# Forgetting attention before the second output projection: values of a head one step later, weight splits in halves, output parts in another order

## What is computed

```python
def fox_mixer(q_raw, k_raw, v_raw, f_raw, f_bias, norm_gain):
    """logit[t,s] = q_t.k_s/sqrt(d) + sum_{s<j<=t} log f_j, s <= t."""
    ...
    def block(i):
        ...
        logits = jnp.einsum('bhtd,bhsd->bhts', qb, k) + (cb[..., :, None] - cum[..., None, :])
        logits = jnp.where(mask, logits, NEG_INF)
        p = jax.nn.softmax(logits, axis=-1)
        return jnp.einsum('bhts,bhsd->bhtd', p, v)
    ...
    o = rms_norm(o, norm_gain)
```

## Time and profile before

| | us |
|---|---|
| median of 3 runs (1623.51 to 1626.19) | 1625.05 |
| the profiled execution | 1622.29 |
| its span | 1621.1 |

### The profile page before, as it was taken

The page is one execution under the profiler, slowest core; times in us unless marked ns, Lnnn a source line. Parts: engine busy times, 40 slices in busy tenths (PEclk is TensorE's granted clock), DMA queues, the critical chain, the costliest instruction groups (busy, mean ns, idle before and its releaser), DMA issues.

```text
span 1621.1 us, 17534 instructions
## 1 busy us (share of the span) xinstructions
PE 1482.9 (91%) x6907; PEld 1160.5 (72%) x6907; DVE 1024.0 (63%) x1354; ACT 756.7 (47%) x995; POOL 121.8 (8%) x143
## 2 busy tenths in 40 slices
PE   6999989889989999999999999999889699999981
PEld 5776668668667787888878787885547578888861
DVE  4888875564325654355546568736434788898976
ACT  5553444644334322122223442254344677887753
POOL 0500000000000000000000303100000011111012
PEclk8989999899999999999999999999999799999996
DMA  6212132202103342322123221111005599999974
GB/s 209 81 67 71 71 130 79 79 28 102 53 26 117 130 137 72 106 104 104 62 72 114 90 93 53 53 53 53 0 1 194 211 374 414 405 411 413 406 294 181
DMA packets 39329, 231.57 MB, mean 143 GB/s; under 512 B 4400, under 2 KB 5696, under 8 KB 17104
## 3 DMA queue, kind: packets, MB, share of 16 engines
q1 hardware_dynamic: 30640, 200.09, 33.0%
q0 software_dynamic: 7648, 27.87, 4.7%
q10 hardware_dynamic: 960, 2.49, 0.4%
HBM read 213.66 MB, written 16.78 MB: 142 GB/s over the span
## 4 chain that ended last, share of the span: by engine, by line
PE 75%; DVE 12%; ACT 6%; issue 4%; DMA 2%; POOL 0%; POOLq 0%; ACTq 0%; DVEq 0%
PE bank L416 15%; PE bank L417 14%; PE bank L418 14%; PE bank L2956 5%; PE bank L2958 5%; PE bank L2957 5%; PE bank L562 3%; DVE w_lo L372 2%; PE bank L435 1%; PE bank L2207 1%; ACT w_hi L366 1%; PE bank L2236 1%; PE bank L437 1%; PE bank L436 1%; PE bank L802 1%
## 5 line engine op out<-in xcount | busy, mean ns | idle before, releaser
L416 PE MATMUL bank<-h_hi,w_hi 128*128 128x512 f32 x952 | 390.5, 410 | 25.8 <-DVE h_lo L496 13.6
L417 PE MATMUL bank<-h_lo,w_hi 128*128 128x512 f32 x952 | 379.9, 399 | 0.0
L418 PE MATMUL bank<-h_hi,w_lo 128*128 128x512 f32 x952 | 379.3, 398 | 0.0
L372 DVE TENSOR_TENSOR w_lo<-w_raw,w_hi 128x2048 fp32r<-128x2048 f32 (+3 forms) x89 | 196.5, 2208 | 96.1 <-ACT w_hi L366 95.5
L416 PEld LDWEIGHTS bank<-h_hi,w_hi 128*128 128x128 f32 x952 | 182.6, 192 | 80.4 <-issue 16.2
L418 PEld LDWEIGHTS bank<-h_hi,w_lo 128*128 128x128 f32 x952 | 182.3, 192 | 42.7
L417 PEld LDWEIGHTS bank<-h_lo,w_hi 128*128 128x128 f32 x952 | 182.6, 192 | 40.6 <-issue 1.9
L366 ACT ACTIVATE w_hi<-w_raw 128x2048 fp32r<-128x2048 f32 (+3 forms) x89 | 158.4, 1780 | 64.8 <-PE bank L418 64.8
L3136 DVE TENSOR_TENSOR h_lo<-w_raw,h_hi 128x2048 fp32r<-128x2048 f32 x32 | 73.3, 2292 | 15.4 <-ACT h_hi L3037 15.4
L3136 DVE TENSOR_TENSOR lo_b<-raw_b,hi_b 128x2048 fp32r<-128x2048 f32 x32 | 73.2, 2288 | 8.7 <-ACT hi_b L3037 8.6
L416 PE MATMUL bank<-a_hi,w_hi 128*128 128x512 f32 x176 | 70.4, 400 | 4.5 <-DVE a_lo L1648 4.5
(11 more groups left out here) (577 smaller groups left out, 2765.1 us busy)
## 6 DMA issues: line engine op xcount, KB each, us to landing
w_raw<-in_params_dram SPq DMA_DIRECT2D x122, 1024.0 KB, 4.9
raw_b<-in_params_dram SPq DMA_DIRECT2D x51, 1024.0 KB, 8.3
w_raw<-in_params_dram SPq DMA_DIRECT2D x16, 704.0 KB, 4.0
result_rows<-osb POOLq DMA_DIRECT2D x16, 512.0 KB, 8.2
result_rows<-prm POOLq DMA_DIRECT2D x8, 512.0 KB, 3.1
xt<-in_x_t_dram POOLq DMA_DIRECT2D x1, 2048.0 KB, 9.3
scratch_rows<-htm SPq DMA_DIRECT2D x4, 512.0 KB, 3.0
out_dram<-pr SPq DMA_DIRECT2D x4, 512.0 KB, 2.6
```

What stands on the lines that cost most here:

```text
L372: V.tensor_tensor(k.w_lo[:, g % SPLIT, 0:size], k.raw[:, g % RAW, 0:size], k.w_hi[:, g % SPLIT, 0:size].bitcast(F32), ALU.subtract).then_i ...
L416: PE.matmul(ps, wh, hi[:, c, 0:width], start=c == 0, stop=False)
L417: PE.matmul(ps, wh, lo[:, c, 0:width], start=False, stop=False)
L418: m = PE.matmul(ps, wl, hi[:, c, 0:width], start=False, stop=c == parts - 1)
```

## The change

- The values of head h (now `pe_fox_out`) move from the end of step 4h + 5 into step 4h + 6, behind that step's scores; those of the last head stand behind one eighth of the output projection, where they had stood ahead of it. What depends on them moves along: ACT's squares and copy of a pair of heads go from the end of step 8j + 9 to step 8j + 10, behind the exponential; PE's sum one step later, ACT's copy of it too.
- Three weight slots are split in two halves, the halves one step apart: `fvb` on DVE (steps 4 and 5; ACT still takes it whole), and the first two slots of `w_out2` on both engines (ACT steps 8, 9 and 19, 20; DVE 10, 11 and 21, 22).
- At the end, ACT takes the exponentials of the first three pairs right after the last `fpt`, ahead of the squares of the last pair; DVE scales three, makes three low parts, and then scales the last. Between exponentials and logarithm ACT's tables are exchanged twice more.
- `pe_w_out2` takes parts in the order (blocks, part) 01:4, 01:5, 01:6, 23:4, 01:7, 23:5, 23:6, 23:7, where it had 01:4 to 01:7 and then 23:4 to 23:7.
- `dve_residual_input(k, 1)` moves from `dve_mix_in` to `dve_hgrn`, ahead of the split of slot `fqb`.

The matmuls, their shapes and all sums are the same.

```diff
+def act_split_half(k, g, half):
+    A, s, n = k.nc.scalar, k.s, SIZES[g] // 2
+    if half == 0:
+        A.wait_ge(k.w_load[g % RAW], 16 * (g // RAW + 1))
+        A.wait_ge(s.gemm, FINAL_BLOCK[g - SPLIT] + 1)
+    m = A.activation(k.w_hi[:, g % SPLIT, half * n:half * n + n], k.raw[:, g % RAW, half * n:half * n + n], ACT.Copy)
+    if half:
+        m.then_inc(s.w_hi, 1)
...
@@ dve_mix_in
     dve_exponents(k, 1)
-    dve_residual_input(k, 1)
     dve_keys(k, 1)
@@ dve_hgrn
     V.tensor_tensor(w1, w1, qf, ALU.mult).then_inc(s.hg_wk, 1)
+    dve_residual_input(k, 1)
     dve_split_to(k, SLOT0["fqb"])
@@ pe_fox
+        if step >= 6 and step % TT == 2:
+            pe_fox_out(k, step // TT - 1)
...
-        if step in (10, 18, 26):
+        if step in (11, 19, 27):
             pe_fox_sum(k, step // 8 - 1)
...
-            if t == TT - 1:
...
-    pe_w_out2_half(k, 12, 2)
+    pe_w_out2_half(k, 12, 1)
+    pe_fox_out(k, FX_H - 1)
+    pe_w_out2_half(k, 13, 1)
+    pe_w_out2_half(k, 14, 1)
     pe_fox_sum(k, 3)
-    pe_w_out2_half(k, 14, 2)
+    pe_w_out2_half(k, 15, 1)
@@ act_fox
+            if step in (10, 18, 26):
+                act_fox_squares(k, step // 8 - 1)
...
-            act_split_to(k, SLOT0["w_out2"] + 1)
-        if step in (11, 19, 27):
+            act_split_half(k, SLOT0["w_out2"] + 1, step - 19)
+        if step in (12, 20, 28):
...
+    a.own()
+    for j in range(3):
+        A.activation(k.grs[:, j, :], k.grs[:, j, :], ACT.Exp, scale=-0.5).then_inc(s.gn_rs, 1)
+    act_fox_squares(k, 3)
+    act_mixed_hi(k, 4)
+    act_mixed_hi(k, 5)
     A.wait_ge(s.gn_sum, 8)
     a(A.activation(k.grs[:, 3, :], k.bank[7][:, :], ACT.Ln, bias=k.eps[:, 0:1], scale=1.0 / HD))
     a.own()
...
+    act_mixed_hi(k, 6)
+    A.activation(k.grs[:, 3, :], k.grs[:, 3, :], ACT.Exp, scale=-0.5).then_inc(s.gn_rs, 1)
     act_mixed_hi(k, 7)
@@ dve_fox
-    dve_fox_scale(k, 0)
-    for j in range(1, 4):
+    for j in range(3):
         dve_fox_scale(k, j)
-        dve_mixed_lo(k, 4 + j - 1)
+    for j in range(3):
+        dve_mixed_lo(k, 4 + j)
+    dve_fox_scale(k, 3)
     dve_mixed_lo(k, 7)
@@ pe_w_out2
-    for b0 in (0, 2):
-        for c in range(4, DB):
+    for b0, c in ((0, 4), (0, 5), (0, 6), (2, 4), (0, 7), (2, 5), (2, 6), (2, 7)):
...
```

More of the change, by code:

```diff
@@ L372, in dve_split, with dve_split_half @@
     V.tensor_tensor(k.w_lo[:, g % SPLIT, 0:size], k.raw[:, g % RAW, 0:size], k.w_hi[:, g % SPLIT, 0:size].bitcast(F32), ALU.subtract).then_inc(s.w_lo, 1)
+def act_split_half(k, g, half):
+    A, s, n = k.nc.scalar, k.s, SIZES[g] // 2
+    assert k.act_slot == g
+    if half == 0:
[4 more added lines that the diff above has]
+        m.then_inc(s.w_hi, 1)
+        k.act_slot += 1
+    else:
+        k.a(m)
+def dve_split_half(k, g, half):
+    V, s, n = k.nc.vector, k.s, SIZES[g] // 2
+    assert k.dve_slot == g
+    if half == 0:
+        V.wait_ge(s.w_hi, g + 1)
+    at = slice(half * n, half * n + n)
+    m = V.tensor_tensor(k.w_lo[:, g % SPLIT, at], k.raw[:, g % RAW, at], k.w_hi[:, g % SPLIT, at].bitcast(F32), ALU.subtract)
+    if half:
+        m.then_inc(s.w_lo, 1)
+        k.dve_slot += 1
+    else:
+        k.v(m)
 def act_split_to(k, g):
@@ L2188, in pe_w_out2_half, with pe_fox_out @@
     pe_fm(k, "w_out2", q // 8, q // 4 % 2, k.hi, k.lo, after="sp", first=q % 4, stop=q % 4 + n)
+def pe_fox_out(k, h):
+    PE, s = k.nc.tensor, k.s
+    r0, blk = HD * (h % 2), h // 2
+    PE.wait_ge(s.sm_pt, SM0 + TT * h + TT)
+    if h % 2 == 0 and blk:
+        PE.wait_ge(s.hg_sig, 6 + blk)
+    if h in (0, 4):
+        PE.wait_ge(s.evac_a, EMPTIED[BLOCK0["fvb" if h else "fva"] + 3][1])
+    for j in range(TT):
+        m = PE.matmul(k.bank[7][r0:r0 + HD, j * P:T], k.fv[:, j, h * HD:h * HD + HD], k.fpt[:, h % 2, j, j * P:T],
+                      start=j == 0, stop=j == TT - 1, skip_group_check=True)
+    m.then_inc(s.fx_o, 1)
 def pe_fox(k):
@@ L2227, in pe_fox @@
             m.then_inc(s.sm_t, 1)
-            if t == TT - 1:
-                r0, blk = HD * (h % 2), h // 2
-                PE.wait_ge(s.sm_pt, SM0 + i + 1)
-                if h % 2 == 0 and blk:
-                    PE.wait_ge(s.hg_sig, 6 + blk)
-                if h in (0, 4):
-                    PE.wait_ge(s.evac_a, EMPTIED[BLOCK0["fvb" if h else "fva"] + 3][1])
-                for j in range(TT):
-                    m = PE.matmul(k.bank[7][r0:r0 + HD, j * P:T], k.fv[:, j, h * HD:h * HD + HD], k.fpt[:, h % 2, j, j * P:T],
-                                  start=j == 0, stop=j == TT - 1, skip_group_check=True)
-                m.then_inc(s.fx_o, 1)
-    pe_w_out2_half(k, 12, 2)
+    pe_w_out2_half(k, 12, 1)
+    pe_fox_out(k, FX_H - 1)
+    pe_w_out2_half(k, 13, 1)
+    pe_w_out2_half(k, 14, 1)
     pe_fox_sum(k, 3)
-    pe_w_out2_half(k, 14, 2)
+    pe_w_out2_half(k, 15, 1)
 def act_fox_squares(k, j):
@@ L2305, in act_fox @@
     a.own()
-    for j in range(4):
-        A.activation(k.grs[:, j, :], k.grs[:, j, :], ACT.Exp, scale=-0.5).then_inc(s.gn_rs, 1)
-        if j:
-            act_mixed_hi(k, 4 + j - 1)
+    act_mixed_hi(k, 6)
+    A.activation(k.grs[:, 3, :], k.grs[:, 3, :], ACT.Exp, scale=-0.5).then_inc(s.gn_rs, 1)
     act_mixed_hi(k, 7)
@@ L2359, in dve_fox @@
                 V.tensor_tensor(in_two(k.hk[:, b, :]), in_two(k.hk[:, b, :]), k.hg[b], ALU.mult).then_inc(s.hg_gate, 1)
[L2360 to L2363 removed]
+        elif step in (4, 5):
+            if step == 5:
+                dve_mix(k, "fkb", 0, k.fk[:, 2, :])
+            dve_split_half(k, SLOT0["fvb"], step - 4)
         elif step in (6, 7, 8):
@@ L2424, in pe_w_out2 @@
     PE, s = k.nc.tensor, k.s
-    for b0 in (0, 2):
-        for c in range(4, DB):
-            for b in (b0, b0 + 1):
-                pe_fm(k, "w_out2", b // 2, b % 2, k.hi, k.lo, first=c, stop=c + 1, after="sp" if b == 0 else None)
-            if b0 and c in (5, 6):
-                pe_w_out2_turn(k, c - 5)
+    for b0, c in ((0, 4), (0, 5), (0, 6), (2, 4), (0, 7), (2, 5), (2, 6), (2, 7)):
+        for b in (b0, b0 + 1):
+            pe_fm(k, "w_out2", b // 2, b % 2, k.hi, k.lo, first=c, stop=c + 1, after="sp" if b == 0 else None)
+        if b0 and c in (5, 6):
+            pe_w_out2_turn(k, c - 5)
     for b in range(4, DB):
```

20 lines of the change are left out of this document (7 added, 13 removed).

## The result

| | before | after |
|---|---|---|
| median, us | 1624.88 (1623.51 to 1626.19, 4 runs) | 1612.86 (1612.35 to 1613.24, 4 runs) |
| the profiled execution | 1622.29 | 1613.24 |
| its span | 1621.1 | 1612.1 |

The ratio is 0.9927, with a 95% interval from 0.9915 to 0.9939: 12 us, 0.7%, faster. The prediction had 1613.6 us, with 1610.5 to 1619.0 as its range. A second series of five runs of the same kernel gave 1611.96 (1611.65 to 1614.94), ratio 0.9934 (0.9920 to 0.9947).

The account below looks back on a forecast made before the run. The prediction took PE, with its idle time between 1095 and 1234 us, as the bound through the attention and behind it. Terms 4.8 + 1.3 + 2.3 + 3.0 = 11.4 us gave 1613.6 us against the median; range 1610.5 to 1619.0.

Parts of the forecast that it names:

- part 4: Residual's scaling moved into HGRN2: DVE's split still waits for ACT's high part, so 0.0 to 0.1 us, counted 0.
- Part 2: Weight slots split in halves in the attention: shorter PE waits for an exponential and a scaled block, 1.3 us recovered.
- the clock at head 4: Products, turns and matmuls behind the shortened waits in the attention: TensorE's clock stays up, returning 2.3 us.
- Part 1: Attention values one step later: seven waits of 0.69 us for ACT's copy `fpt` go, 4.8 us.
- rival 2: Softmax chain in the attention replaces the waits removed by later values; total gain 6.6 us, 1618.5 us; chance 0.08.
- Rival 1: Clock falls behind the attention's two shorter idles and for all of turn and pair; gain 8.1, 1617.0 us; chance 0.17.
- Part 3: End of attention and output projection reordered: the 3.5 us low-part wait goes, a 2.2 us wait comes; 3.0 us gained.
- the 1065: DVE's state in HGRN2: coming later than 1065 us was named as a sign of a wrong prediction.
- Rival 3: Pause behind each of three ACT table loads at the end; total gain 7.6 us, 1617.4 us; chance 0.03.
- Rival 4: PE held at 1.2 GHz through much of attention and projection; slower, 1634 us for 40 us of it; chance 0.03.

Follow-up runs that it names:

- e5: Changed kernel with DVE's wait for the norm row and its first product moved behind block 1's add and the third slot's split: 1607.65 us, ratio 0.9889.
- e6: Changed kernel with the first expert's three loads held back until the norm row has landed: 1612.04 us, one run.
- e8: Changed kernel with the end's old orders restored, the last head's values still behind one eighth of the projection: 1613.70 us, ratio 0.9939.
- e3: Kernel before with only the new orders at the end of the attention and in the output projection: 1621.07 us, ratio 0.9981.
- e4: Kernel before with only the residual's scaling moved: 1623.63 us, one run.
- e7: Changed kernel with the three weight slots whole again: 1616.49 us, ratio 0.9953.
- e9: Changed kernel with DVE's later wait for the norm row and ACT's second output-weight slot in quarters instead of halves: 1606.35 us, ratio 0.9893.
- e10: Changed kernel with ACT's second output-weight slot in quarters instead of halves, the norm row's wait unmoved: 1608.69 us, ratio 0.9910.

## Why the prediction was right, and where it wasn't

**The sum** was 11.4 us; the medians differ by 12.0, with an interval from 9.9 to 13.8. The number came out better than its terms, and part of that is luck. The profiles of the kernel after show 9.5 us for the attention, 0.1 for the end and 0.6 for part 4, 10.2 in all, in the first, and 6.3, 1.8 and 0.6, 8.7 in all, in the second. Part 2 and part 4 gave more than their terms, the end less, and the clock at head 4 its full term in one profile and not in the other. The medians can't tell 8.7 or 10.2 from 11.4: the second series has 8.6 to 13.0 as its interval. The three parts alone gave 4.7, 4.5 and 3.2 us by their medians, 12.4 together, each known to about 1.6 us, and 3.5, 4.4 and 1.8 in their profiles, 9.8 together. That agrees with a plain sum, and would not show an overlap of 2 us.

**Part 1** (4.8 us): right. The seven waits went, with 4.7 us measured for the part alone (3.5 in its profile, with the longer low clock). The softmax chain (rival 2) has not shown: the walk's slack of 0.2 us was enough.

**Part 2** (1.3 us): the kind was right, one term too low. I had 0.6 and 1.0 us of waits left, which is 1.4 and not 1.3 us recovered; it was 0.56 and 0.57, so 1.9 us came back. ACT needs 1.42 us from the start of the second half to that exponential (1164.42 to 1165.84), close to the 1.5 I had counted; the walk had 0.4 us too much elsewhere, and where I have not traced.

**The clock at head 4** (2.3 us): right in the profile of the kernel after, but the step behind it was not. I had argued that idles of 1.63 and 1.70 us had been followed by full speed, so two shorter ones would be too. The second profile, e5, e6 and e8 show two idles of 0.56 and 0.57 us, 1.6 us of work apart, with the clock down behind the second, at 3.2 us. With both idles gone it stayed up. The length of one idle is not what decides. The bound between 1.70 and 1.94 us, which I had read from the earlier trace rows, was chance: at the place of the 1.94 all fourteen profiles have an idle of 1.93 to 1.98 us, and the work behind it took 5.44 us in nine, in part at half clock, and its 3.81 us of full clock in five (e3, e4, e7, e9, e10; the lines of e4 and e10 stand under the table of all profiles). Behind an idle of 2.5 us at the next such place it took 3.81 us in two (e9, e10) and 5.44 in three (e3, e4, e7). Rival 1, at 0.17, is what these executions did at this place, and it deserved more. The Trainium skill, in "TensorE: Matmul & The Clock Gate", section "A second HAM failure mode: psum-queue depth-cycling", tells of a bf16 kernel whose frequent short idles between groups of matmuls let the clock go up and down. Four of the five profiles with the two waits agree, with 0.56 and 0.57 us; the fifth stayed at full clock.

**Part 3** (3.0 us): the mechanism was right, two terms were mis-sized, the row's landing and the price of the low clock. ACT's walk held: low part 7 stood at 13.1 us behind the start of the last turn (1219.2 - 1206.09) and DVE ended it at 13.0 (1210.05 + 0.69 - 1197.71); the wait for part 7 was 0.37 us instead of 0.6. The row was taken at 7.0 us from the earlier trace rows and took 8.5, so PE's wait for the second turn was 3.46 instead of 2.2: 1.3 us lost. The price of the low clock behind it, 1.6 by my estimate, was 1.35 in e3, e7, e10 and the second profile (third turn 5.74 us behind the second instead of the 4.39 it takes at full clock without a wait) and 2.8 in the first (7.17). That leaves 3.0 - 1.3 + 0.25 = 1.9 us, as these four profiles have it (33.8 - 32.0), and next to nothing in the first. Its execution gained 3.2 us at head 4 and gave back 1.7 at the end, against the second one.

**Part 4** (0): the split stayed behind ACT, as I had it, but its term was 0.6 us too low. I had asked only when the split starts and taken its length as given; it ran 0.58 us faster with no residual ahead of it, and 0.6 us reached the first scores. The margin at the state was 1.16 us in the kernel after, 1.0 by the prediction. The state itself came at 1065.86, later than the 1065 I had named as a sign of being wrong. That says nothing against the part: this execution was 1.6 us later already at the instruction of 969.90 (971.50), and measured from there the state came 0.5 us sooner.

**Rival 3**, a pause behind the table loads, did not come. ACT's time line of the kernel after:

```profile
1198.99 1.28 ACT L2343 ACT_TABLE_LOAD   x1
1200.28 1.67 ACT L2343 ACTIVATE hk<-hk 128x512 f32<-128x512 f32 x3
...
1203.98 1.28 ACT L2348 ACT_TABLE_LOAD   x1
1205.27 0.69 ACT L2348 ACTIVATE hk<-bank,eps 128x512 f32<-128x512 f32 x1
```

Each load starts within 0.02 us of the end of the work ahead of it, and the next function 0.01 to 0.02 us behind its 1.28 us. The drain of some 1.38 us that the Trainium skill gives in "ScalarE: Activation LUTs", section "What ACT_TABLE_LOAD costs", is not in this trace either.

**Rival 4** did not come. In the attention of the kernel after, ahead of head 4, PE is busy without a break and the granted clock is 1.00:

```profile
1120.00:1163.00 43.00, 43.00 (x212) 27.68 (x211) 22.62 (x71) 18.21 (x49) 0.00 (x0) 1.00 0.08 25
```

The 0.92 from 1225 to 1240 us is the tail of the low clock behind the second turn's wait.

**What stays open**: why the row is slower with the new end, why the low clock behind one and the same wait lasts some 3.4 us in four profiles and some 6.8 in one (mean granted clock 0.83 and 0.66 over the 10 us around it), what decides in an execution whether it comes behind one and the same idle at all, and where the 6.3 us of scatter ahead of HGRN2 come from.

## What to carry to other kernels

When an edit makes an engine reach a wait earlier, ask what is queued behind that wait and whether it needs it: here one wait for a row stood ahead of an add that PE wanted, and moving it shortened the end by 4 us and more, where the new order alone had brought 2. Short idles close to each other can cost as much as one of some microseconds, through TensorE's clock, so clear them in pairs and look at more than one profile before you count the clock as won. A bound on the length of such an idle that is read from one profile is no bound: here the same 1.9 us went either way. Before you take an instruction's length as given, look at what runs beside it on another engine. And take the landing time of a DMA from the loads that will run beside it.
